# A fused transformer forward pass on one Trainium2 core: four transpositions of normalised rows, with the scale inside TensorE's product or in VectorE's copy

## The chip, the core and the metric

The kernel runs as one program on one core of one Trainium2 chip. The core has a matrix engine (TensorE, PE in the profile, with its weight loads listed apart as PEld), VectorE (DVE), ScalarE (ACT), GpSimd (POOL), and SyncE (SP), whose queue issues the transfers. Each engine runs its own list of instructions in order; semaphores tie the lists together. The metric is the device time of one execution in microseconds, lower is better. In this kernel about 0.2%, some 4 us, is what a measurement can tell from no change.

## The reference, cut to what matters

The program computes a first block (a mixer of convolutions and gates, cross attention, a mixture of 32 experts) and then a second block of two layers, for 256 tokens of width 1024, all in fp32. The four places that the change touches are the four RMS norms of the second block:

```python
def second_block(x, c, ada_w, ada_b, norm_gains, ...):
    for layer in range(2):
        shift_m, scale_m, gate_m, shift_f, scale_f, gate_f = ada_mod(c, ada_w[layer], ada_b[layer])
        h = modulate(rms_norm(x, norm_gains[layer, 0]), shift_m, scale_m)   # h0, h2
        y = attn_hybrid_mixer(h, ...) if layer % 2 == 0 else retention_mixer(h, ...)
        x = x + gate_m * y
        h = modulate(rms_norm(x, norm_gains[layer, 1]), shift_f, scale_f)   # h1, h3
        x = x + gate_f * swiglu(h, ffn_w_gate_up[layer], ffn_w_down[layer])
    return rms_norm(x, final_norm)
```

rms_norm divides every row (token) by the root of its mean square and multiplies by a gain per column; modulate multiplies by a factor and adds a shift per column.

## The kernel before, in words

The tokens lie in `x_tok`, 128 partitions by two row blocks i = 0, 1 by 1024 columns. The product after a norm needs the normalised tokens transposed: 8 chunks of 128 features on the partitions, 256 tokens along the free axis. This step is called a turn. There are seven: `t_mem`, `t_1`, `t_2` in the first block, and `t_h[0]` to `t_h[3]` (h0 to h3 here) at the part boundaries of the second block. Each turn is four groups, group 2i + h: row block i, half h of the columns, four 128x128 tiles in one PSUM bank.

`t_mem`, `t_1` and `t_2` turn rows that VectorE has normalised, by `pe.transpose` (L1089). h0 to h3 turn the rows of `x_tok` as they are and scale them in the same step: VectorE multiplies the identity by the column `inv[:, i]` of inverse roots (`scale_diag`, L2413, 128x128), and TensorE multiplies each tile by this diagonal matrix (L1087). The compiled fp32 product is two passes, 16 records in the trace for 8 tiles; a transposition has one.

Around it, at h1, h2 and h3, the list of each engine is this. VectorE, for the last block of tokens i: gate the product (L3037), add it to `x_tok` (L3042). ScalarE: the squares of the new half with their sum (L1751), the root (L1760). VectorE: the reciprocal (L2401), the diagonal (L2413). TensorE: the 8 tiles of block i. Then the turned tiles are read out of PSUM with the gain as factor and the shift added: ScalarE takes half h = 0 of block 0 (`turn_out`, L1772), VectorE half h = 1 (L2420). ScalarE makes the fp32r high part of h = 0 (L1713), VectorE the rest (L2319). Of block 1 ScalarE writes the high part of h = 0 straight from PSUM (`turn_out_last`, L1788), VectorE that of h = 1 (L2430). The first product of the next part (`first_units`, L978) takes ScalarE's chunks one by one as they land. L2312 and L1703 split weights into low and high parts and stand between these steps in both lists.

At h0 the rows come from the experts' sum: `finish_rows(i)` (L2867) writes `x_tok`, ScalarE takes the squares of whole rows (L1749) and the root, and in ScalarE's list a weight split (L1703) stands between the two row blocks. There ScalarE makes both high pieces of block 0 (L1713, twice), the second of which needs VectorE's L2420, before L1788.

TensorE waits for `tok_ready`, which VectorE raises by one for each row block. The turned tiles wait in banks `front`, freed by `evac`. Where `finish_rows` and `scale_diag` stand in VectorE's list is written out by hand at L2870 to L2877 for h0, and in `turn_scaled` (L3052) for the others.

Of the kernel before, what the change touches and what calls it, by code (L numbers as in the profile page):

```python
# [22 lines left out]
ALU = mybir.AluOpType  # L23
# [7 lines left out]
TT = T // P  # L31
# [162 lines left out]
def build_program(nc, a, consts1, consts2, decay, params, rows, gates_out, out):  # L194
    with ExitStack() as ctx:
# [5 lines left out]
        def sem(name):  # L201
            if name not in sems:
                sems[name] = ctx.enter_context(nc.semaphore(name))
            return sems[name]
# [45 lines left out]
        def big(i):  # L250
            return arena[:, i * DC * T:(i + 1) * DC * T].rearrange("p (c t) -> p c t", c=DC)
# [8 lines left out]
        def k1(name, n=P):  # L260
            return c1[:, C1[name]:C1[name] + n]

        ident = k1("ident")
        def tokens(i):
            return arena[:, i * DC * T:(i + 1) * DC * T].rearrange("p (i f) -> p i f", i=TT)

        x_tok, mem_tok = tokens(0), tokens(1)
# [107 lines left out]
        turn_h = [plan.turn()]  # L375
# [128 lines left out]
        def at(t):  # L504
            return ring[t.slot]
# [95 lines left out]
        inv, warm = small[:, 30:32], small[:, 63:64]  # L601
# [82 lines left out]
        def piece(x, k, pieces):  # L684

            if pieces == 1:
                return x
            if pieces == 2:
                n = x.shape[1] // 2
                return x[:, n * k:n * (k + 1), :]  # L690
            return x[:, 4 * (k % 2):4 * (k % 2) + 4, P * (k // 2):P * (k // 2 + 1)]
# [37 lines left out]
        def cols(name):  # L729
            return lambda c: pc(name, c)  # L730
# [3 lines left out]
        def mcol(layer, j):  # L734
            return lambda c: mod[:, 48 * layer + DC * j + c:48 * layer + DC * j + c + 1]

        def scol(k):
            return lambda c: gscale[:, DC * k + c:DC * k + c + 1]
# [1 line left out]
        t_mem = Turn(turn_mem, mem_tok, cols("mem_ln_g"), cols("mem_ln_b"), memT)  # L740
        t_1 = Turn(turn_1, tokens(8), cols("ln1_g"), cols("ln1_b"), x1T)
        t_2 = Turn(turn_2, tokens(8), cols("ln2_g"), cols("ln2_b"), x2T)
        inv_diag = [k1("before"), k1("slot")]
        t_h = [Turn(turn_h[k], x_tok, scol(k), mcol(k // 2, 3 * (k % 2)), big(6), inv_diag) for k in range(4)]

        def turned_part(t, i, h):

            g = t.block.groups[2 * i + h]
            return g, [(t.dst[:, 4 * h + k, P * i:P * (i + 1)], bank[g % BANKS][:, P * k:P * (k + 1)], 4 * h + k)
                       for k in range(4)]  # L750
# [203 lines left out]
        def _(pe):  # L954
            def open_group(g):
                if g >= BANKS:

                    pe.wait_ge(evac[g % BANKS], g // BANKS)
                return bank[g % BANKS]
# [115 lines left out]
            def turn(t, between=None):  # L1075

                for i in range(TT):
                    if i and between:
                        between()
                    pe.wait_ge(sem("tok_ready"), TT * t.n + i + 1)  # L1080
                    for h in range(2):
                        turned = open_group(t.block.groups[2 * i + h])
                        for k in range(4):
                            c = 4 * h + k
                            x, dst = t.src[:, i, c * P:(c + 1) * P], turned[:, k * P:(k + 1) * P]
                            if t.scale:
                                mm = pe.matmul(dst, x, t.scale[i], start=True, stop=True)  # L1087
                            else:
                                mm = pe.transpose(dst, x, ident)  # L1089
                        mm.then_inc(sem("mm_done"), 1)  # L1090

            def norm_mean(n):
# [70 lines left out]
            for k, g in enumerate(pool_groups):  # L1163
                dst = open_group(g)
                for i in range(TT):
                    for kc in range(2):
                        mm = pe.matmul(dst[:, i * T:(i + 1) * T], pool_in[:, 2 * k + kc, i * P:(i + 1) * P],
                                       at(pool_tile)[:, 2 * k + kc, 0:T], start=kc == 0, stop=kc == 1)
# [55 lines left out]
            for h in range(XHEADS):  # L1224
                wait_evac(pe, xq[h // 2].groups[h % 2])
                for i in range(TT):
                    for k in range(2):
                        mm = pe.matmul(bank[h][:, i * T:(i + 1) * T], qT[:, 2 * h + k, i * P:(i + 1) * P],
                                       kT[:, 2 * h + k, :], start=k == 0, stop=k == 1)
# [43 lines left out]
            def logits(i):  # L1273
# [3 lines left out]
                for k in range(DC):  # L1277
# [13 lines left out]
                      stop=True).then_inc(sem("r_pos"), 1)  # L1291
# [125 lines left out]
            for i in range(TT):  # L1417
                mm = pe.matmul(bank[5][0:NEXP, i * P:(i + 1) * P], gates[:, i, :], ident, start=True, stop=True)
# [875 lines left out]
        def _(dve):  # L2294
# [8 lines left out]
            V = nc.vector  # L2303
# [11 lines left out]
            def split_low(name, which=None):  # L2315
                first, pieces, src, high, low = splits[name]
                for k in which or range(pieces):
                    dve.wait_ge(sem("x_high"), first + k + 1)
                    V.tensor_tensor(piece(low, k, pieces), piece(src, k, pieces), piece(high, k, pieces).bitcast(F32),  # L2319
                                    ALU.subtract).then_inc(sem("x_split"), 1)  # L2320
# [76 lines left out]
            def invert(i):  # L2397

                inverses[0] += 1
                dve.wait_ge(sem("std"), inverses[0])  # L2400
                link(V.reciprocal(inv[:, i:i + 1], inv[:, i:i + 1]))  # L2401
# [5 lines left out]
                return V.tensor_scalar(dst[:, i, :], src[:, i, :], moments[:, i, 0:1], inv[:, i:i + 1],  # L2407
                                       ALU.subtract, ALU.mult)

            def scale_diag(t, i):  # L2410

                invert(i)
                V.tensor_scalar(t.scale[i], ident, inv[:, i:i + 1], None, ALU.mult).then_inc(sem("tok_ready"), 1)  # L2413

            def turn_out(t, i):

                g, parts = turned_part(t, i, 1)
                dve.wait_ge(sem("mm_done"), plan.done[g])
                for dst, ps, c in parts:
                    ins = V.tensor_scalar(dst, ps, t.g(c), t.b(c), ALU.mult, ALU.add)  # L2420
                ins.then_inc(evac[g % BANKS], 1)
# [293 lines left out]
            slot = k1("slot")  # L2715
# [71 lines left out]
            for q in range(4):  # L2787
                i, f = q // 2, slice((q % 2) * 512, (q % 2 + 1) * 512)
# [70 lines left out]
            def centre_late():  # L2859

                invert(1)
                link(V.scalar_tensor_tensor(out=acc[:, 1, :], in0=pair[1][:, :], scalar=late_neg, in1=g3,
                                            op0=ALU.add, op1=ALU.mult))

            def finish_rows(i):

                V.scalar_tensor_tensor(out=x_tok[:, i, :], in0=acc[:, i, :], scalar=inv[:, i:i + 1], in1=b3,  # L2867
                                       op0=ALU.mult, op1=ALU.add).then_inc(sem("resid"), 1)
# [2 lines left out]
            invert(0)  # L2871
            finish_rows(0)
            centre_late()
            scale_diag(t_h[0], 0)
            finish_rows(1)
            scale_diag(t_h[0], 1)
            turn_out(t_h[0], 0)  # L2877
            low_until(units_of(aq[0])[0])
            split_low("h0", (0,))
# [172 lines left out]
            def turn_scaled(t, name):  # L3052

                def then(i):
                    scale_diag(t, i)
                    if i:
                        turn_out(t, 0)
                        split_low(name, (0,))
                        turn_out_last(t, name)
                        split_low_last(t, name)  # L3060

                return then
# [245 lines left out]
```

## Time and profile before

| what | value |
|---|---|
| median of 3 runs | 2090.04 us |
| lowest and highest | 2089.27 and 2093.59 us |
| the profiled execution's own time | 2092.46 us |
| its span | 2090.7 us |
| PE busy in the span | 2022.1 us, 97% |
| DVE, ACT busy | 1126.7 us (54%), 708.4 us (34%) |
| mean granted clock of TensorE | 0.998 of full speed |

The span is the time between the first and the last instruction of the profiled execution; 1.8 us of its own time lie around it. The four boundaries lie at 1364 (h0), 1493 (h1), 1684 (h2) and 1892 us (h3). A granted clock (PEclk) of 1.00 is 2.4 GHz, 0.50 is 1.2 GHz. Ends of matmuls are modelled, and instructions of one engine overlap a little, so the start of the next may come before the end of the last.

### The profile page before, as it was taken

The numbers are of one execution on the slowest core, as the hardware profiler recorded it, in microseconds if no ns is written. First come the engines' busy times: TensorE is split into PE (matmuls) and PEld (weight loads), VectorE is DVE, ScalarE is ACT, GpSimd is POOL, SyncE is SP. The second block draws the span as 40 slices with busy tenths as digits, with TensorE's granted clock in tenths as the row PEclk, the third lists the DMA queues.
The fourth block names the chain that finished last, engine by engine and source line by source line (L and its number), as shares of the span: only waits on it lengthen the run. The fifth ranks groups of instructions, "written<-read, shape, count | busy, mean of one in ns | idle before, by whom it ended". The sixth has DMA issues, their size and how long they took to land.

```text
span 2090.7 us, 28509 instructions
## 1 busy us (share of the span) xinstructions
PE 2022.1 (97%) x11518; PEld 1339.9 (64%) x11518; DVE 1126.7 (54%) x1732; ACT 708.4 (34%) x937; POOL 3.1 (0%) x10
## 2 busy tenths in 40 slices
PE   8999999999999999999999999999999999999998
PEld 7999998853333333333333333388788898888887
DVE  6998898642222222221222222268798676657764
ACT  4334554521111111111111111175555443545543
POOL 0000000000000000000000000000000000000000
PEclk9999999999999999999999999999999999999999
DMA  9544759999999999999999999963488756646752
GB/s 340 190 170 174 282 200 368 364 392 396 429 428 427 428 428 429 429 428 429 427 429 428 428 429 427 419 234 111 150 289 283 262 189 215 211 161 202 249 173 81
DMA packets 188011, 654.91 MB, mean 313 GB/s; under 512 B 10992, under 2 KB 76528, under 8 KB 162704
## 3 DMA queue, kind: packets, MB, share of 16 engines
q1 hardware_dynamic: 187920, 653.59, 80.3%
q8 instruction: 71, 1.16, 0.2%
q14 instruction: 20, 0.16, 0.0%
HBM read 652.50 MB, written 1.06 MB: 313 GB/s over the span
## 4 chain that ended last, share of the span: by engine, by line
PE 74%; DMA 21%; DVE 3%; ACT 1%; issue 0%; SPq 0%; ACTq 0%; DVEq 0%
DMA ring<-w_down 21%; PE front L1020 19%; PE front L1071 15%; PE front L1322 10%; PE pair L1350 7%; PE front L1041 5%; PE pair L1041 2%; PE front L1043 2%; PE front L978 2%; PE pair L1390 1%; PE pair L1302 1%; PE pair L1043 1%; PE front L1332 1%; DMA ring<-w_in 1%; DVE ring_low L2312 1%; PE pair L1310 1%
## 5 line engine op out<-in xcount | busy, mean ns | idle before, releaser
L2312 DVE TENSOR_TENSOR ring_low<-ring,w_high 128x2048 fp32r<-128x2048 f32 (+1 forms) x179 | 404.6, 2266 | 133.0 <-ACT w_high L1703 132.5
L1322 PE MATMUL front<-ring,arena 128*64 128x512 f32 x1808 | 403.4, 595 | 9.9 <-DMA ring<-w_gu 9.7
L1703 ACT ACTIVATE w_high<-ring 128x2048 fp32r<-128x2048 f32 (+1 forms) x179 | 338.1, 1893 | 176.8 <-PE front L1071 77.9
L1020 PE MATMUL front<-x_parts,w_high 128*128 128x256 f32 x2048 | 373.5, 285 | 11.0 <-DVE ring_low L2512 9.1
L2808 DVE TENSOR_TENSOR arena<-front,par 128x512 f32<-128x512 f32 x64 | 44.0, 687 | 621.5 <-PE front L1332 621.5
L1020 PEld LDWEIGHTS front<-x_parts,w_high 128*128 128x128 f32 x2048 | 321.2, 193 | 14.7 <-issue 11.7
L1322 PEld LDWEIGHTS front<-ring,arena 128*64 128x64 f32 x1808 | 125.7, 137 | 278.3 <-issue 243.6
L1020 PE MATMUL front<-x_parts,ring_low 128*128 128x256 f32 x1024 | 290.6, 284 | 0.0
L1071 PE MATMUL front<-w_high,arena_r 128*128 128x512 f32 x736 | 229.2, 390 | 1.3 <-DVE ring_low L2312 0.7
L1350 PE MATMUL pair<-ring,arena 128*64 128x512 f32 x864 | 195.3, 597 | 27.5 <-DMA ring<-w_down 27.5
L1020 PEld LDWEIGHTS front<-x_parts,ring_low 128*128 128x128 f32 x1024 | 197.3, 193 | 0.0
L1071 PEld LDWEIGHTS front<-w_high,arena_r 128*128 128x128 f32 x736 | 138.2, 188 | 32.3 <-issue 3.1
L1350 PEld LDWEIGHTS pair<-ring,arena 128*64 128x64 f32 x864 | 59.3, 136 | 145.1 <-issue 145.1
L1041 PE MATMUL front<-x_parts,w_high 128*128 128x512 f32 x416 | 147.3, 398 | 0.0
L1071 PE MATMUL front<-ring_low,arena_r 128*128 128x512 f32 x368 | 143.3, 389 | 0.0
L1043 PE MATMUL front<-x_parts,ring_low 128*128 128x256 f32 x416 | 116.7, 280 | 0.0
L2017 ACT ACTIVATE arena<-front 128x512 f32<-128x512 f32 x64 | 34.7, 595 | 232.1 <-PE front L1322 232.1
L2362 DVE SCALAR_TENSOR_TENSOR arena<-a_pad,par,arena 128x256 f32<-128x256 f32 x240 | 98.5, 482 | 0.3
L2006 ACT ACTIVATE arena<-pair 128x512 f32<-128x512 f32 x32 | 19.1, 597 | 231.0 <-PE pair L1302 231.0
L1041 PEld LDWEIGHTS front<-x_parts,w_high 128*128 128x128 f32 x416 | 78.1, 188 | 20.4 <-issue 1.7
L2032 ACT ACTIVATE arena<-pair 128x512 f32<-128x512 f32 x30 | 17.9, 597 | 214.1 <-PE pair L1350 214.1
L1041 PE MATMUL pair<-x_parts,w_high 128*128 128x512 f32 x224 | 79.3, 397 | 0.0
(373 smaller groups left out, 2359.6 us busy)
## 6 DMA issues: line engine op xcount, KB each, us to landing
ring<-w_gu SPq DMA_DIRECT2D x113, 2048.0 KB, 23.6
ring<-w_down SPq DMA_DIRECT2D x57, 2048.0 KB, 25.4
ring<-ffn_w_gate_up SPq DMA_DIRECT2D x44, 1024.0 KB, 7.7
ring<-ada_w SPq DMA_DIRECT2D x20, 2048.0 KB, 8.7
ring<-ret_w_in SPq DMA_DIRECT2D x12, 2048.0 KB, 8.0
ring<-w_in SPq DMA_DIRECT2D x10, 2048.0 KB, 7.9
arena<-w_gu SPq DMA_DIRECT2D x10, 2048.0 KB, 15.4
ring<-ffn_w_down SPq DMA_DIRECT2D x8, 2048.0 KB, 8.3
```

The source lines that it names most:

```text
L978: mm = pe.matmul(acc_bank[:, ch * T:(ch + 1) * T], w[:, k, ch * P:(ch + 1) * P], xs[:, k, :], start=start and k + ch == 0, stop=stop and k ...
L1020: mm = pe.matmul(acc_bank[:, ch * T:(ch + 1) * T], w[:, k, ch * P:(ch + 1) * P], xs[:, kk, :], start=kk + ch + n == 0, stop=kk == b.kc - 1 ...
L1041: pe.matmul(both, high[:, k, cols], x_parts[:, :, k, :], start=k == 0, stop=False, skip_group_check=True)
L1043: mm = pe.matmul(sums[:, ch, :], low[:, k, cols], x[0][:, k, :], start=False, stop=k == b.kc - 1, skip_group_check=True)
L1071: mm = pe.matmul(acc_bank[:, :], xs[:, kk, i * P:(i + 1) * P], w[:, k, :], start=kk + n == 0, stop=kk == b.kc - 1 and n == 2)
L1322: mm = pe.matmul(bank[b][64 * o:64 * o + 64, :], xgT[:, k // 4, k % 4, :], gu_cols(b_in, j, D * o + 512 * b), start=k == 0, stop=k == DC - 1)
L1350: mm = pe.matmul(dst[64 * o:64 * o + 64, :], actT[:, k, :], down_cols(b_in, j, 512 * o), start=k == 0, stop=k == DC - 1)
L1703: nc.scalar.activation(high_part(u), raw_part(u), ACT.Copy).then_inc(sem("w_high"), 1)
L2017: nc.scalar.activation(gu_s[b], bank[b][:, :], ACT.Copy).then_inc(sem("m_gus"), 1)
L2312: V.tensor_tensor(low_part(u), raw_part(u), high_part(u).bitcast(F32), ALU.subtract).then_inc(sem("w_low"), 1)
L2362: V.scalar_tensor_tensor(out=conv[:, c, :], in0=a_pad[:, c, tap:tap + T], scalar=pc("conv_a_w", tap * DC + c), in1=conv[:, c, :], op0=ALU. ...
L2808: V.tensor_tensor(tv, bank[first + b][:, :].rearrange("p (c j) -> p c j", c=8), bias, ALU.add).then_inc(sem("m_vec"), 1)
```

## The change

The four boundaries turn scaled rows. `scale_rows` in place of `scale_diag` multiplies a row block of `x_tok` by `inv` into `tokens(2)`, in two halves of 512 columns, and raises `tok_ready` after each; `rows_ready` gives TensorE the count that it waits for before each group, and TensorE turns every tile by `pe.transpose`. At h0 `finish_rows(1)` moves ahead of both scalings. At h1, h2 and h3 VectorE's `turn_out(t, 0)` moves ahead of the scaling of block 1.

```diff
-        inv_diag = [k1("before"), k1("slot")]
-        t_h = [Turn(turn_h[k], x_tok, scol(k), mcol(k // 2, 3 * (k % 2)), big(6), inv_diag) for k in range(4)]
+        t_h = [Turn(turn_h[k], tokens(2), scol(k), mcol(k // 2, 3 * (k % 2)), big(6), x_tok) for k in range(4)]
+
+        def rows_ready(t, i, h):
+
+            if t.scale is None:
+                return TT * t.n + i + 1
+            return TT * t_h[0].n + 2 * TT * (t.n - t_h[0].n) + 2 * i + h + 1
...
-                    pe.wait_ge(sem("tok_ready"), TT * t.n + i + 1)
                     for h in range(2):
+                        pe.wait_ge(sem("tok_ready"), rows_ready(t, i, h))
                         turned = open_group(t.block.groups[2 * i + h])
...
-                            if t.scale:
-                                mm = pe.matmul(dst, x, t.scale[i], start=True, stop=True)
-                            else:
-                                mm = pe.transpose(dst, x, ident)
+                            mm = pe.transpose(dst, x, ident)
...
-            def scale_diag(t, i):
+            def scale_rows(t, i):
 
                 invert(i)
-                V.tensor_scalar(t.scale[i], ident, inv[:, i:i + 1], None, ALU.mult).then_inc(sem("tok_ready"), 1)
+                for h in range(2):
+                    cols = slice(512 * h, 512 * (h + 1))
+                    V.tensor_scalar(t.src[:, i, cols], t.scale[:, i, cols], inv[:, i:i + 1], None,
+                                    ALU.mult).then_inc(sem("tok_ready"), 1)
...
             centre_late()
-            scale_diag(t_h[0], 0)
             finish_rows(1)
-            scale_diag(t_h[0], 1)
+            scale_rows(t_h[0], 0)
+            scale_rows(t_h[0], 1)
             turn_out(t_h[0], 0)
...
                 def then(i):
-                    scale_diag(t, i)
                     if i:
                         turn_out(t, 0)
+                    scale_rows(t, i)
+                    if i:
                         split_low(name, (0,))
```

How this stands in VectorE's list at h0, from the row block 1 of the experts' rows to the weight split behind the turn. The names after the arrow are the tiles read; `c` holds the constants and the diagonals, `small` the inverse roots, `front` the turned tiles. Before:

```order
L2862 SCALAR_TENSOR_TENSOR arena<-pair,small,arena 128x1024 [waits dve_step]
L2401 RECIPROCAL small<-small 128x1 [waits std,dve_step]
L2413 TENSOR_SCALAR c<-c,small 128x128 [waits dve_step]
L2867 SCALAR_TENSOR_TENSOR arena<-arena,small 128x1024
L2401 RECIPROCAL small<-small 128x1 [waits std]
L2413 TENSOR_SCALAR c<-c,small 128x128 [waits dve_step]
L2420 TENSOR_SCALAR arena<-front,gscale,mod 128x128 [waits mm_done]
L2420 TENSOR_SCALAR arena<-front,gscale,mod 128x128 x3
L2312 TENSOR_TENSOR ring_low_52<-ring,w_high_53 128x8x256 [waits w_high]
```

and now (the lines of the changed kernel are three to six further down, L2418 is the scaling, L2873 `finish_rows`, L2426 `turn_out`, L2315 the weight split):

```order
L2868 SCALAR_TENSOR_TENSOR arena<-pair,small,arena 128x1024 [waits dve_step]
L2873 SCALAR_TENSOR_TENSOR arena<-arena,small 128x1024 [waits dve_step]
L2404 RECIPROCAL small<-small 128x1 [waits std]
L2418 TENSOR_SCALAR arena<-arena,small 128x512 [waits dve_step]
L2418 TENSOR_SCALAR arena<-arena,small 128x512
L2404 RECIPROCAL small<-small 128x1 [waits std]
L2418 TENSOR_SCALAR arena<-arena,small 128x512 [waits dve_step]
L2418 TENSOR_SCALAR arena<-arena,small 128x512
L2426 TENSOR_SCALAR arena<-front,gscale,mod 128x128 [waits mm_done]
L2426 TENSOR_SCALAR arena<-front,gscale,mod 128x128 x3
L2315 TENSOR_TENSOR ring_low_52<-ring,w_high_53 128x8x256 [waits w_high]
```

`finish_rows` stands ahead of the first reciprocal, and two copies of 128x512 for each row block stand where one of 128x128 did; ahead of `turn_out` there are now both copies of block 1.

VectorE's list at h1, from the addition of block 1 to the high part of its half. Before:

```order
L3042 TENSOR_TENSOR arena<-arena 128x512 [waits evacuated0]
L2401 RECIPROCAL small<-small 128x1 [waits std]
L2413 TENSOR_SCALAR c<-c,small 128x128 [waits dve_step]
L2420 TENSOR_SCALAR arena<-front,gscale,mod 128x128 [waits mm_done]
L2420 TENSOR_SCALAR arena<-front,gscale,mod 128x128 x3
L2319 TENSOR_TENSOR x_parts<-arena,x_parts 128x4x128 [waits x_high]
L2430 TENSOR_SCALAR x_parts<-front,gscale,mod 128x128 [waits x_split,mm_done]
```

and now (L3048 is the addition, L2322 the low part, L2436 the high part):

```order
L3048 TENSOR_TENSOR arena<-arena 128x512 [waits evacuated0]
L2426 TENSOR_SCALAR arena<-front,gscale,mod 128x128 [waits mm_done]
L2426 TENSOR_SCALAR arena<-front,gscale,mod 128x128 x3
L2404 RECIPROCAL small<-small 128x1 [waits std]
L2418 TENSOR_SCALAR arena<-arena,small 128x512 [waits dve_step]
L2418 TENSOR_SCALAR arena<-arena,small 128x512
L2322 TENSOR_TENSOR x_parts<-arena,x_parts 128x4x128 [waits x_high]
L2436 TENSOR_SCALAR x_parts<-front,gscale,mod 128x128 [waits x_split,mm_done]
```

The four reads out of PSUM stand ahead of the reciprocal and the scalings. h2 and h3 have the same rows with other bank numbers. TensorE's list has the same 16 tiles in the same order at each boundary, with a wait for `tok_ready` before each group of four in place of one before each eight.

## Rows read from the trace of the kernel before

**Rows 1.** The page, busy time (share of the span) of each engine, TensorE and VectorE
```profile
PE 2022.1 (97%) x11518; PEld 1339.9 (64%) x11518; DVE 1126.7 (54%) x1732; ACT 708.4 (34%) x937; POOL 3.1 (0%) x10
```

**Rows 2.** Chain of waits, 1492 to 1500: start us, us, what
```profile
1496.10 2.05 PE front L1087 x16
1498.15 1.91 PE front L978 x12
```

**Rows 3.** Timeline, boundary h1: start us, us, engine, line, operation [idle before <-releaser]
```profile
1492.83 1.95 PE L1087 MATMUL front<-c,arena 128*128 128x128 f32 x16
...
1493.75 0.69 DVE L3042 TENSOR_TENSOR arena<-arena 128x512 f32<-128x512 f32 x1
...
1495.43 1.49 ACT L1772 ACTIVATE arena<-front,mod,gscale 128x128 f32<-128x128 f32 x4
1495.56 0.16 DVE L2401 RECIPROCAL small<-small 128x1 f32<-128x1 f32 x1 [1.11 <-ACT small L1760]
...
1496.10 2.05 PE L1087 MATMUL front<-c,arena 128*128 128x128 f32 x16 [1.33 <-DVE c L2413]
1497.01 0.63 ACT L1713 ACTIVATE x_parts<-arena 128x512 fp32r<-128x512 f32 x1
1497.55 1.49 ACT L1788 ACTIVATE x_parts<-front,mod,gscale 128x128 fp32r<-128x128 f32 x4
...
1498.13 1.46 PE L978 MATMUL front<-x_parts,w_high 128*128 128x256 f32 x8
1498.28 1.36 DVE L2430 TENSOR_SCALAR x_parts<-front,gscale,mod 128x128 fp32r<-128x128 f32 x4
```

**Rows 4.** Timeline, boundary h2
```profile
1689.11 1.50 ACT L1788 ACTIVATE x_parts<-front,mod,gscale 128x128 fp32r<-128x128 f32 x4
...
1689.69 1.47 PE L978 MATMUL front<-x_parts,w_high 128*128 128x256 f32 x8
```

**Rows 5.** Timeline, the turn t_1 and the products before it
```profile
347.93 1.92 PE L1119 MATMUL pair<-ring,silu_c 128*32 128x512 f32 x16
...
351.80 1.09 PE L1089 MATMUL front<-c,arena 128*128 128x128 f32 x8
```

**Rows 6.** Line L3129: duration ns min/median/max, first and last start, form
```profile
L3129 DVE TENSOR_SCALAR arena<-arena,small x2: 485/487/489, 2083.0 to 2087.0; 128x512 f32<-128x512 f32 x2
```

**Rows 7.** Timeline, boundary h0
```profile
1367.19 0.29 DVE L2413 TENSOR_SCALAR c<-c,small 128x128 f32<-128x128 f32 x1
1367.39 1.36 DVE L2420 TENSOR_SCALAR arena<-front,gscale,mod 128x128 f32<-128x128 f32 x4
...
1368.44 1.15 ACT L1713 ACTIVATE x_parts<-arena 128x512 fp32r<-128x512 f32 x2
1368.67 2.29 DVE L2312 TENSOR_TENSOR ring_low<-ring,w_high 128x2048 fp32r<-128x2048 f32 x1
1369.50 1.49 ACT L1788 ACTIVATE x_parts<-front,mod,gscale 128x128 fp32r<-128x128 f32 x4
...
1370.08 1.46 PE L978 MATMUL front<-x_parts,w_high 128*128 128x256 f32 x8 [0.50 <-ACT x_parts L1788]
```

**Rows 8.** Chain of waits, boundary h0
```profile
1368.98 0.61 ACT x_parts L1713
```

**Rows 9.** Stretches around turn t_2: busy of each engine, PEclk, DMA share, GB/s
```profile
436.00:440.00 4.00, 4.00 (x25) 4.00 (x24) 2.81 (x4) 1.44 (x2) 0.00 (x0) 0.60 1.00 426
440.00:443.00 3.00, 3.00 (x17) 1.45 (x21) 1.80 (x13) 0.00 (x0) 0.00 (x0) 0.50 1.01 426
443.00:446.00 3.00, 3.00 (x21) 1.79 (x14) 2.72 (x10) 1.02 (x3) 0.00 (x0) 0.90 0.95 322
```

**Rows 10.** Timeline of PE, turn t_2 and the router's products
```profile
433.95 1.09 PE L1089 MATMUL front<-c,arena 128*128 128x128 f32 x8 [0.42 <-DVE arena L2407]
435.32 5.67 PE L1278 MATMUL pair<-par,arena 128*128 128x32 f32 x32 [0.28 <-DVE arena L2420]
440.92 3.24 PE L1119 MATMUL pair<-ring,silu_c 128*32 128x512 f32 x16
```

## Prediction

> **What bounds the kernel now.** I began with the busy shares on the page: TensorE is busy for 97% of the span [rows 1]. So a change pays only where it makes TensorE start earlier or work less, and at the four boundaries the question is who lets it start again. The chain of waits at h1 runs through the add of block 1, its squares and root, the reciprocal and the diagonal into TensorE's 16 passes, 2.05 us, and from these straight into the first product L978 [rows 2]. By the chain alone, those passes are on the path.
>
> The timeline beside it says otherwise. ScalarE's row of the same moments is closed: the four reads of block 0 start at 1495.43, the high part at 1497.01, the four high chunks of block 1 at 1497.55, and L978 at 1498.13 [rows 3]. L978 starts 0.58 us after ScalarE's L1788. At h2 it is 1689.69 - 1689.11 = 0.58 [rows 4], and at h0, where TensorE does stand idle for ScalarE and is therefore surely not the last, 1370.08 - 1369.50 = 0.58 [rows 7]. The same distance where TensorE is free and where the chain blames it means that ScalarE is the last link at h1 and h2 too, and TensorE's passes end level with it by chance. I read h3 as h2. So at each boundary the path is: add, squares, root, then 2.7 us of ScalarE reads (1495.43 to 1498.13 at h1). Nothing in the change shortens these.
>
> **The change part by part.**
>
> *TensorE's tiles.* A group of 8 tiles takes 1.95 to 2.05 us as products of two passes [rows 3]; 8 transpositions take 1.09 us [rows 5]. Removed work: 8 groups x 0.9 to 0.96, about 7.5 us of busy time. What of it is on the path? The first group of each boundary ends at 1494.78 before and TensorE then waits 1.33 us for block 1 [rows 3]; it will only wait longer. The second group starts when block 1 is scaled and must be half done when ScalarE comes to it at 1497.55, and wholly done at 1498.13. Both hold now. Worth: 0, and between 0 and 0.96 us at each of h1 to h3 if my reading of ScalarE is wrong.
>
> *VectorE's copies at h1 to h3.* The diagonal of 128x128 goes, two copies of 128x512 come. The same form is in L3129, 0.49 us [rows 6]. For block 0: reciprocal, two copies, done about 0.7 us later than the diagonal was, still before TensorE finishes the last product of the part at 1492.8. Hidden. For block 1: VectorE's add ends at 1493.75 + 0.69 = 1494.44 [rows 3]. Now its four reads (1.36 us, the form at 1367.39 [rows 7]) come first and end about 1495.75, where it would else have idled 1.11 us [rows 3]. The reciprocal, before at 1495.56, moves to about 1495.65. First copy done at 1496.35, second at 1496.85. Half a group of transpositions is 0.6 us: the first four tiles are ready at 1497.0, the others at 1497.4. ScalarE wants the first at 1497.55, VectorE the others at 1498.28, TensorE wants to be free at 1498.13. Spare: 0.5, 0.8 and 0.7 us. Worth: 0; the cover is gone when a copy takes over 0.49 + 0.25 us.
>
> *VectorE at h0.* Here the reads stand behind the copies. `finish_rows(1)` moves 0.6 us forward, but the squares of block 1 stand behind a weight split in ScalarE's list, so the second reciprocal stays at 1367.0. Before, the diagonal starts at 1367.19 and the reads at 1367.39, a step of 0.20 [rows 7]. Two copies step 0.40 to 0.49 each, so the reads start 0.6 to 0.8 us later, at 1368.0 to 1368.2, and end 1369.35 to 1369.55. ScalarE's second high piece, 1368.98 before [rows 8], needs them: it slips by 0.4 to 0.6 us, and with it L1788 and L978. The weight split L2312 slips by the same 0.6 to 0.8 from its 1368.67, ends near 1371.6, and the products that need it start near 1371.85. Cost: +0.4 to +0.6, taken +0.5. If ScalarE is then still later than I think it is 0; if VectorE's high chunks (4 x 0.34) come late as well, +0.8.
>
> *Waits.* Each group of four tiles has its own wait, 14 more in seven turns, all on a count that in `t_mem`, `t_1` and `t_2` has already been reached. Behind them stand only TensorE's own tiles. A step over a semaphore takes up to 0.09 us (L1772 ends at 1496.92, L1713 starts at 1497.01 [rows 3]), so between 0 and 14 x 0.09 = 1.3 us; the count being reached already, taken 0. SP's and the other queues wait for the same `mm_done` counts and lose nothing.
>
> *TensorE's clock.* The removed passes were work that TensorE did in the gap. After the change it does, between the last product at 1492.83 and L978 at 1498.13, two groups of 1.09 us in 5.3 us, where it did 4.0 us; at h0 about 2.2 in 6.5. One place of the trace before resembles this: the turn `t_2`. TensorE turns 8 tiles at 433.95, waits 0.28 us, then does narrow products (32 columns) from 435.32 [rows 10], and the granted clock falls in 436 to 440 (mean 0.60), is 0.50 in 440 to 443 and 0.90 in 443 to 446 [rows 9]. That is 3.2 + 3.0 + 0.6 = 6.8 us at 1.2 GHz. It came back 2.7 us after wide products had begun again at 440.92 [rows 10]. Turn `t_1`, with products of 512 columns around its transpositions, kept 2.4 GHz. The price of the low level: the 16 products of L1119 take 3.24 us at 440.92 and 1.92 us at 347.93 [rows 5, 10], 1.32 lost in some 2.7 low, 0.49 us per us. After a boundary the products are wide at once, so what matters is the low time behind L978: from 0 to those 6.8 us, 0 to 3.3 us per fall. I take 1.5 us low, under the 2.7 of the row since part of it lies before L978: 0.7 us. And I take it at three of four boundaries, +2.1.
>
> On this the Trainium skill has a sentence (TensorE: Matmul & The Clock Gate, Part 4: PE-mode transpose): a transposition does not count as PE-busy the way a product does. It speaks against this change, and `t_2` agrees with it [rows 9, 10], though the narrow products stand there as well. By the page all four boundaries would look idle to the gate: four falls, +2.8 in place of +2.1.
>
> **The sum.** h1 to h3 0; h0 +0.5; waits 0; clock +2.1; together +2.6 us. The profiled execution took 2092.46 us, 1.8 over its span of 2090.7, so a like one gives 2095.1. It stands 2.4 above the median of 2090.04; on that median the forecast is 2092.6.
>
> **The rivals.**
>
> 1. *The clock stays up.* For it: no gap of TensorE at a boundary is as empty as the router's stretch is long, and in the trace before the clock holds at all four. Against: the removed passes are what held it. Then only h0's +0.5 remains, 2090.5.
>
> 2. *Slower: the clock falls at all four and stays low as long as in rows 9.* Place: the products behind L978. Price 6.8 x 0.49 = 3.3 us each, 13.3 + 0.5, 2103.9. It decides, that is passes 4 us in all, from 1.8 us low behind L978 at each boundary. For it: that length is the only one that the trace shows within the program. Against: there TensorE stayed on narrow products for 5.67 of the 6.8 us.
>
> 3. *Faster: the chain is right.* The passes of block 1 are the last link at h1, h2 and h3, and L978 starts as much earlier as they shrink, 3 x 0.96 = 2.9 us less, h0's +0.5 kept: 2087.6. For it: the chain of waits, which shows no idle time before L978. Against: 0.58 us three times. A further gain cannot come, since the root of block 1 does not move.
>
> 4. *The copies don't hold their place.* A 128x512 copy that took 0.8 us instead of 0.49 would bring the first tiles of block 1 at 1497.3 and the others at 1498.0: still just hidden at h1 to h3, but +1.2 at h0: 2091.2.
>
> **How the numbers follow.** The forecast with falls at some boundaries 0.50; rival 1 0.27; rival 2 0.11, most of it well under its full price; rival 3 0.07; rival 4 0.05. A difference under 0.2%, 4.2 us, can't be told from none here. Rival 3 reaches faster only with the spread of the runs (2089.27 to 2093.59), so faster gets 0.06. Rival 2 is slower, and the forecast with long falls gives a little: slower 0.15. Same 0.79. The range must hold that spread of 4.3 us around terms of -2.4 to +6: 2088.0 to 2096.8; rival 2 at its full price is left out.
>
> **What would show it.** Right: L978 starts 0.58 us after L1788 at all four boundaries, and in h1 to h3 L1788 starts as long after the add as before (3.8 us); TensorE shows two idle gaps per boundary, the longer about 2.5 us; at h0 ScalarE's second high piece waits for VectorE's reads and L978 comes 0.5 us later after the weight split; PEclk is below 1.00 in some of the stretches behind a boundary. Wrong: L1788 or L978 nearer to the add by half a microsecond (rival 3), PEclk 1.00 throughout (rival 1), or ScalarE or VectorE waiting for a group of block 1 at h1 to h3 (copies slower than taken). The forecast as a whole is wrong if the median moves by over 4 us in either direction.

## The result, and the profile after

| kernel | runs | median us | ratio to before, 95% interval |
|---|---|---|---|
| before | 17 | 2090.04 (2088.67 to 2093.59) | |
| changed | 17 | 2094.65 (2090.70 to 2096.42) | 1.0020 (1.0013 to 1.0026) |

The change made the kernel 4.6 us, 0.22%, slower. That is just above the 0.2% that I set as the bound of "same", over the 4 us at which I had called the forecast as a whole wrong, and inside the range. The profiled execution took 2092.84 us (span 2091.0, mean granted clock 0.995; before 2092.46, 2090.7 and 0.998).

TensorE has fewer passes, as intended. The page of the changed kernel, against [rows 1]:

```profile
PE 2017.0 (96%) x11454; PEld 1334.1 (64%) x11454; DVE 1131.1 (54%) x1740; ACT 709.0 (34%) x937; POOL 3.1 (0%) x10
```

5.1 us less busy time, and a longer run. The timeline at h1, which answers to [rows 3] (the lines are three to six further down; the columns are the same):

```profile
1491.09 1.03 PE L1092 MATMUL front<-c,arena 128*128 128x128 f32 x8
...
1492.02 0.69 DVE L3048 TENSOR_TENSOR arena<-arena 128x512 f32<-128x512 f32 x1
...
1494.09 0.88 DVE L2418 TENSOR_SCALAR arena<-arena,small 128x512 f32<-128x512 f32 x2
...
1494.63 1.09 PE L1092 MATMUL front<-c,arena 128*128 128x128 f32 x8 [2.51 <-DVE arena L2418]
...
1495.82 1.49 ACT L1791 ACTIVATE x_parts<-front,mod,gscale 128x128 fp32r<-128x128 f32 x4
...
1496.40 1.46 PE L984 MATMUL front<-x_parts,w_high 128*128 128x256 f32 x8 [0.67 <-ACT x_parts L1791]
```

From the add (L3048) to the first product (L984) it is 1496.40 - 1492.02 = 4.38 us. Before it was 1498.13 - 1493.75 = 4.38. TensorE now stands idle for 2.51 us where it did for 1.33. The chain of waits over the same stretch no longer names TensorE's tiles (start, us, what), against [rows 2]:

```profile
1493.79 1.41 ACT arena L1775 x4
...
1495.82 0.45 ACT x_parts L1791
...
1496.40 1.70 PE front L984 x10
```

With the passes gone the chain goes through ScalarE's reads, and the end of it has not moved. At h1 to h3 the difference is behind the first product. The granted clock is the number ahead of the last two (DMA share and GB/s); stretches of h0 (two), h1, h2 and h3:

```profile
1364.00:1370.00 6.00, 5.03 (x22) 4.66 (x23) 6.00 (x13) 5.60 (x14) 0.00 (x0) 0.51 1.05 389
1370.00:1376.00 6.00, 6.00 (x49) 6.00 (x48) 6.00 (x9) 2.85 (x2) 0.00 (x0) 0.92 0.55 220
1498.00:1504.00 6.00, 6.00 (x52) 6.00 (x52) 6.00 (x9) 4.31 (x6) 0.00 (x0) 1.00 0.13 39
1690.00:1696.00 6.00, 6.00 (x46) 6.00 (x45) 6.00 (x8) 2.61 (x4) 0.00 (x0) 0.85 0.01 4
1898.00:1904.00 6.00, 6.00 (x45) 6.00 (x44) 6.00 (x12) 5.44 (x9) 0.00 (x0) 0.83 0.33 106
```

Before, all five read 1.00. Now the clock is at 1.2 GHz for (1 - 0.51) x 2 x 6 = 5.9 us and 1.0 us more at h0, 6.8 in all, for none at h1, and for 3.4 us each at h2 and h3 (from stretches of 1 us). What it costs shows in how far the block of 48 products lies behind the first product: the distance at full clock is 4.17 to 4.18 us before. At h2 after:

```profile
1687.39 1.49 ACT L1791 ACTIVATE x_parts<-front,mod,gscale 128x128 fp32r<-128x128 f32 x4
...
1687.97 1.83 PE L984 MATMUL front<-x_parts,w_high 128*128 128x256 f32 x8 [0.67 <-ACT x_parts L1791]
...
1693.43 5.92 PE L984 MATMUL front<-x_parts,w_high 128*128 128x256 f32 x48
```

and before, whose first product is in [rows 4]:

```profile
1693.87 5.92 PE L978 MATMUL front<-x_parts,w_high 128*128 128x256 f32 x48
```

5.46 us against 4.18: 1.28 lost, and the first product still 0.58 us behind ScalarE's L1791. At h0, against [rows 7]:

```profile
1364.16 1.97 PE L1092 MATMUL front<-c,arena 128*128 128x128 f32 x8 [1.00 <-DVE arena L2418]
...
1365.82 0.63 ACT L1716 ACTIVATE x_parts<-arena 128x512 fp32r<-128x512 f32 x1 [0.31 <-DVE arena L2426]
1366.36 1.49 ACT L1791 ACTIVATE x_parts<-front,mod,gscale 128x128 fp32r<-128x128 f32 x4
...
1366.94 2.05 PE L984 MATMUL front<-x_parts,w_high 128*128 128x256 f32 x8 [0.81 <-ACT x_parts L1791]
...
1372.59 5.92 PE L984 MATMUL front<-x_parts,w_high 128*128 128x256 f32 x48
```

and before:

```profile
1374.25 5.99 PE L978 MATMUL front<-x_parts,w_high 128*128 128x256 f32 x48
```

ScalarE's second high piece waited 0.31 us for VectorE's reads. From the start of `finish_rows(0)` (1357.43 now, 1360.87 before) to the first product it is 9.51 us where it was 9.21, so 0.30 lost; from there to the 48 products 5.65 where it was 4.17, 1.48 lost. About 0.1 of the 1.48 is not the clock's: in e5 and e8 below, whose clock stays up at h0, that distance is 4.26 and 4.28. The clock fell at 1364.1, ahead of the second group, which took 1.97 us where the first took 1.09. Of this one profile:

| | h0 | h1 | h2 | h3 | sum |
|---|---|---|---|---|---|
| first product later | 0.30 | 0 | 0 | 0 | 0.30 |
| products behind it slower | 1.48 | 0 | 1.28 | 0.83 | 3.59 |

3.9 us. The span grew by only 0.3 mostly because the experts' stage ended 3.4 us earlier in this execution (L1368's last products at 1352.5, L1365's before at 1355.9), 1.9 of it already at its start: the clock, low for 6.8 us at `t_2` in [rows 9], was low for half of that here (PEclk 0.88 in 436 to 440, 0.58 in 440 to 443). That stage varies from run to run by itself.

### The profile page after: what moved, and what is told of

Same layout as the page of the kernel before. It is cut to its first block, busy times and chain, and to the rows that moved or that the text cites. A ratio compares the mean times of both kernels' runs of the same rounds, so it can differ in the third digit from the quotient of the medians.

```text
span 2091.0 us, 28402 instructions
## 1 busy us (share of the span) xinstructions
PE 2017.0 (96%) x11454; PEld 1334.1 (64%) x11454; DVE 1131.1 (54%) x1740; ACT 709.0 (34%) x937; POOL 3.1 (0%) x10
## 4 chain that ended last, share of the span: by engine, by line
PE 74%; DMA 21%; DVE 2%; ACT 1%; issue 0%; SPq 0%; ACTq 0%; DVEq 0%
DMA ring<-w_down 21%; PE front L1026 19%; PE front L1077 15%; PE front L1325 10%; PE pair L1353 7%; PE front L1047 5%; PE pair L1047 2%; PE front L984 2%; PE front L1049 2%; PE pair L1393 1%; PE pair L1305 1%; PE pair L1049 1%; PE front L1335 1%; DMA ring<-w_in 1%; DVE ring_low L2315 1%; PE pair L1122 1%
## 5 line engine op out<-in xcount | busy, mean ns | idle before, releaser
L2315 DVE TENSOR_TENSOR ring_low<-ring,w_high 128x2048 fp32r<-128x2048 f32 (+1 forms) x179 | 404.7, 2267 | 137.3 <-ACT w_high L1706 136.8
```

What stands on the lines that cost most here:

```text
L2315: V.tensor_tensor(low_part(u), raw_part(u), high_part(u).bitcast(F32), ALU.subtract).then_inc(sem("w_low"), 1)
```

## The experiments

Theory 1: TensorE's clock falls, since the removed passes leave it too little to do between the two parts. Theory 2: VectorE's copies and their new place cost the time. All times are medians; each ratio is to runs of the kernel before on the same chip, whose medians were 2090.23 (beside e1 to e8), 2089.90 (e9 to e11) and 2089.64 us (e12). The low times are those of the one profiled execution.

| kernel | median | ratio (95%) | clock low at h0, h1, h2, h3, us |
|---|---|---|---|
| e1_products | 2094.28 | 1.0020 (1.0011 to 1.0029) | 0, 3.4, 0, 3.4 |
| e2_raw_turn | 2095.45 | 1.0020 (1.0011 to 1.0030) | 6.8, 3.4, 3.4, 6.8 |
| e3_fill | 2094.07 | 1.0016 (1.0007 to 1.0025) | none |
| e4_fill_h0 | 2093.68 | 1.0016 (1.0007 to 1.0025) | none |
| e5_fill_fit | 2090.27 | 1.0001 (0.9992 to 1.0010) | none |
| e6_fill_fit_h0 | 2089.84 | 1.0001 (0.9992 to 1.0010) | none |
| e7_early_reads | 2088.77 | 0.9993 (0.9984 to 1.0002) | none |
| e8_products_order | 2091.83 | 1.0009 (1.0000 to 1.0018) | none |
| e9_early_one_fill | 2088.29 | 0.9991 (0.9982 to 1.0000) | none |
| e10_turn_fill | 2092.14 | 1.0014 (1.0003 to 1.0026) | none |
| e11_changed_again | 2094.98 | 1.0020 (1.0011 to 1.0029) | 6.8, 0, 3.4, 6.8 |
| e12_turn_fill_again | 2092.92 | 1.0018 (1.0006 to 1.0031) | none |

**e2: the transpositions alone.** The kernel before with one line changed; the norm's scale is left out of the result.

```diff
-                                mm = pe.matmul(dst, x, t.scale[i], start=True, stop=True)
+                                mm = pe.transpose(dst, x, ident)
```

> The kernel before with VectorE's list untouched (the diagonal is still made and waited for), but TensorE turns the unscaled rows by transposition at the four boundaries; the norm's scale is left out of what is computed. Theory 1: the clock falls at two to four boundaries, +2.5 to +4.5 us over before, 2092.5 to 2094.5, though nothing was added to VectorE. Theory 2: TensorE's shorter tiles cost nothing, 2090.0; by the chain of waits (TensorE's passes last at h1 to h3) it would be 2.9 us less, 2087.1.

Measured 2095.45, 5.2 us over before and above the range that I gave theory 1, with VectorE's list untouched. TensorE stood idle for 2.24 us between the groups at h1 to h3, where the kernel before has 1.33. The first product stands 4.38 us behind the add at h1, h2 and h3 (4.39), as before; the clock falls at all four boundaries. The stretches behind h2 and at h3:

```profile
1690.00:1696.00 6.00, 6.00 (x39) 5.95 (x39) 6.00 (x12) 4.38 (x8) 0.00 (x0) 0.72 0.30 111
1898.00:1904.00 6.00, 5.06 (x26) 4.85 (x24) 5.65 (x15) 5.89 (x13) 0.00 (x0) 0.54 0.64 209
```

From first product to the 48 it is 6.04, 4.48, 5.51 and 6.56 us against 4.17 to 4.18: 5.9 us lost in the profile. At h1 only 0.31 was lost, since 2.2 of the 3.4 us at the low clock lay before the first product. Theory 2 gave 2090.0 and is out as the main cause, and the chain's promise of 2087.1 too.

The clock was lower in the other executions too, not only in the profiled ones: its mean over an execution was 0.993 to 0.997 (median 0.994) in the 17 of the changed kernel and in the 10 of e2, and 0.996 to 0.999 (median 0.998) in those of the kernel before beside the experiments. The shortest of each, 2090.70 and 2090.09 us, are the ones with 0.997.

**e1: the copies, with products.** The tiles of h0 to h3 as two-pass products with the identity, the rest as changed.

```diff
-                            mm = pe.transpose(dst, x, ident)
+                            if t.scale is None:
+                                mm = pe.transpose(dst, x, ident)
+                            else:
+                                mm = pe.matmul(dst, x, ident, start=True, stop=True)
```

> The changed kernel with its scaled copies and its order in VectorE's list, but at the four boundaries TensorE turns the tiles by a two-pass product with the identity in place of a transposition. Theory 1 (the time was lost because TensorE's clock falls when its tiles in the gap are transpositions): no fall at any boundary, each L978-like first product 0.57 to 0.58 us behind ScalarE's first high chunk; only the later start at h0, 0.3 us, stays: 2090.0 to 2091.0 us where before is 2090.0. Theory 2 (the copies and their order cost the time): unchanged against the changed kernel, about 2094.6.

A miss: 2094.28, which by itself is what theory 2 forecast. But the experiment had a fault of its own, which its timeline at h1 shows:

```profile
1489.15 1.95 PE L1095 MATMUL front<-c,arena 128*128 128x128 f32 x16
...
1491.14 1.37 DVE L2429 TENSOR_SCALAR arena<-front,gscale,mod 128x128 f32<-128x128 f32 x4 [0.37 <-PE front L1095]
...
1493.15 3.28 PE L1095 MATMUL front<-c,arena 128*128 128x128 f32 x16 [2.05 <-DVE arena L2421]
...
1494.76 1.50 ACT L1794 ACTIVATE x_parts<-front,mod,gscale 128x128 fp32r<-128x128 f32 x4 [0.79 <-PE front L1095]
...
1496.08 1.67 PE L984 MATMUL front<-x_parts,w_high 128*128 128x256 f32 x8
```

VectorE's reads, now ahead of the scaling, wait 0.37 us for the longer group of block 0 and make the scaling late; TensorE idles 2.05 us, the clock falls although its tiles are products, and the second group takes 3.28 us where it took 2.05. The first product is 6.00 us behind the add (4.88 at h2, which did not fall, and 5.35 at h3). So products in the group are not enough; the empty time between the groups matters as well.

**e8: the same with the old order.** As e1, and `scale_rows` ahead of `turn_out` at h1 to h3.

```diff
                 def then(i):
+                    scale_rows(t, i)
                     if i:
                         turn_out(t, 0)
-                    scale_rows(t, i)
-                    if i:
                         split_low(name, (0,))
```

> The scaled copies of the changed kernel with two-pass products with the identity in place of the transpositions, and at h1 to h3 the order of the kernel before (the scaling ahead of turn_out). In the run with products and the new order TensorE waited 2.05 us for block 1 and the clock fell at h1 and h3; with the old order it waits about 1.5 us. Theory 1: no fall, the copies alone cost 0.2 to 0.3 us at each boundary since TensorE's two-pass group becomes the last link: 2090.8 to 2091.6. Theory 2: 2094.

```profile
1493.06 2.05 PE L1095 MATMUL front<-c,arena 128*128 128x128 f32 x16 [1.53 <-DVE arena L2421]
...
1494.31 1.49 ACT L1794 ACTIVATE x_parts<-front,mod,gscale 128x128 fp32r<-128x128 f32 x4
...
1494.89 1.46 PE L984 MATMUL front<-x_parts,w_high 128*128 128x256 f32 x8
```

No fall, idle time 1.53 us, the first product 4.38 us behind the add: the copies cost nothing at h1 to h3, even ahead of the reads. The profile accounts for 0.4 us at h0 (0.30 to the first product, 0.11 behind it); the median is 1.6 up with an interval that begins at 1.0000, so the rest isn't settled.

**e3, e4: the gaps filled, too long.** Unread products behind each row block's tiles.

```diff
                         mm.then_inc(sem("mm_done"), 1)
+                    if t.scale is not None:
+                        for _ in range(1 if i else 2 if t is t_h[0] else 5):
+                            pe.matmul(bank[4], ident, c1[:, 0:COLS], start=True, stop=True)
```

> The changed kernel, and behind each row block's transpositions at h0 to h3 TensorE does products of 128x512 that nobody reads, into a bank that is free: 5 behind block 0 (2 at h0), 1 behind block 1, 2.15 us and 0.43 us in gaps of 2.5 and 0.67 us. Theory 1: the clock stays at 2.4 GHz at h1 to h3, and perhaps at h0, where less fits: 2090.3 if at all four, 2091.7 if h0 still falls. Theory 2: no less than the changed kernel, 2094.6, and more where a product overlaps the start of the next part.

> As the filled kernel, and at h0 VectorE's reads out of PSUM (turn_out) stand ahead of the scaling of block 1, as at the other boundaries. Both theories: ScalarE's second high piece no longer waits for VectorE, so the first product at h0 starts 0.4 us earlier, slightly ahead of the kernel before (0.1 us). Theory 1: 2089.9 us together. Theory 2: 2094.2.

Both miss, 2094.07 and 2093.68, and both keep the clock at all four boundaries:

```profile
1493.69 4.46 PE L1096 MATMUL pair<-c 128*128 128x512 f32 x10
...
1497.98 1.04 PE L1092 MATMUL front<-c,arena 128*128 128x128 f32 x8
...
1498.62 1.50 ACT L1794 ACTIVATE x_parts<-front,mod,gscale 128x128 fp32r<-128x128 f32 x4 [0.99 <-PE front L1092]
...
1499.32 1.52 PE L984 MATMUL front<-x_parts,w_high 128*128 128x256 f32 x8
```

A 512-column product takes 0.89 us, twice what I had reckoned (I counted one of its two passes), and five of them hold TensorE to 1498.15. The first product is 5.57 to 5.58 us behind the add, 1.2 later at each of three boundaries, 3.6 us: what the clock gave back went there. In e4, which also has the change at h0 that e6 has, the first product there comes 0.32 us earlier than in the changed kernel.

**e5, e6: the gaps filled to measure.** 256 columns in place of 512; e6 also moves `turn_out` ahead of `scale_rows(t_h[0], 1)` at h0.

```diff
-                            pe.matmul(bank[4], ident, c1[:, 0:COLS], start=True, stop=True)
+                            pe.matmul(bank[4][:, 0:T], ident, c1[:, 0:T], start=True, stop=True)
```

> The changed kernel with shorter unread products behind the transpositions: 256 columns each, two passes of 0.22 us, 5 behind block 0 (2 at h0) and 1 behind block 1. The 512-column ones of the first try took 0.89 us each, 4.46 us for five, and held TensorE past its second group. Theory 1 (the clock): these end within the gaps of 2.51 and 0.67 us, the clock stays at 2.4 GHz at all four, L984 stands 4.38 us behind the add at h1 to h3 as before, and only h0's later start stays: 2090.0 to 2091.2. Theory 2 (copies and order, not the clock): 2094 as before.

```profile
1492.24 2.32 PE L1096 MATMUL pair<-c 128*128 128x256 f32 x10
...
1494.91 1.09 PE L1092 MATMUL front<-c,arena 128*128 128x128 f32 x8 [0.35 <-DVE arena L2421]
...
1496.09 1.49 ACT L1794 ACTIVATE x_parts<-front,mod,gscale 128x128 fp32r<-128x128 f32 x4
...
1496.67 1.46 PE L984 MATMUL front<-x_parts,w_high 128*128 128x256 f32 x8 [0.23 <-ACT x_parts L1794]
```

```profile
1364.00:1370.00 6.00, 4.63 (x31) 3.70 (x30) 4.96 (x10) 5.57 (x15) 0.00 (x0) 1.00 1.05 386
1690.00:1696.00 6.00, 6.00 (x52) 6.00 (x51) 6.00 (x9) 2.88 (x5) 0.00 (x0) 1.00 0.03 11
1898.00:1904.00 6.00, 6.00 (x52) 6.00 (x52) 6.00 (x9) 4.33 (x6) 0.00 (x0) 1.00 0.14 44
```

2090.27, against 2090.23 of the kernel before on its chip: of the changed kernel's 4.6 us nothing is left that can be told from chance (the interval allows 2 us either way). TensorE idles 0.35 us before its second group, the clock reads 1.00, and every copy, wait and reordering of the change is still in. This is the run that shows the cause, with e2 as its mirror. Its mean clock is 0.997 to 0.999 (median 0.998) in its 11 runs, as before.

> As the kernel with fitted products, and at h0 VectorE's reads stand ahead of the scaling of block 1. Theory 1: 0.3 us less, level with the kernel before, 2089.7 to 2090.7. Theory 2: 2094.

2089.84. At h0 the first product stands 9.09 us behind `finish_rows(0)`, 0.42 less than in the changed kernel and 0.12 less than before; the 48 products behind it stand 13.57 us from there, where it was 13.38, since VectorE's later steps now come late. The medians differ by 0.4, which they can't tell from chance; the profile can.

**e7, e9: a version that uses the shorter tiles.** e7 is e6, and ScalarE does three reads of block 0 ahead of the squares of block 1; e9 is e7 without the unread product behind block 1 at h1 to h3.

```diff
             def turn_rms(t, name):
 
+                turn_out(t, 0, range(3))
                 sum_squares(1, 1)
                 rms_root(1)
-                turn_out(t, 0)
+                turn_out(t, 0, (3,))
```

> As that one, and ScalarE does three of its four reads of block 0 (turn_out) at h1 to h3 ahead of the squares of block 1, in the 1.2 us in which it waits for VectorE's add. My reading that ScalarE is the last link: its list after the root shrinks by 3 x 0.37 us, then the second group's transpositions bound it, so the first product starts 0.5 us earlier at h1, h2 and h3, 1.5 us in all: about 2088.6. If VectorE and TensorE are the last link: no gain, 2090.2.

```profile
1493.11 1.16 ACT L1778 ACTIVATE arena<-front,mod,gscale 128x128 f32<-128x128 f32 x3 [0.21 <-PE front L1092]
...
1493.39 0.69 DVE L3053 TENSOR_TENSOR arena<-arena 128x512 f32<-128x512 f32 x1
...
1495.10 0.44 ACT L1778 ACTIVATE arena<-front,mod,gscale 128x128 f32<-128x128 f32 x1
...
1496.01 1.09 PE L1092 MATMUL front<-c,arena 128*128 128x128 f32 x8 [0.35 <-DVE arena L2423]
...
1496.70 1.51 ACT L1796 ACTIVATE x_parts<-front,mod,gscale 128x128 fp32r<-128x128 f32 x4 [0.44 <-PE front L1092]
...
1497.31 1.46 PE L984 MATMUL front<-x_parts,w_high 128*128 128x256 f32 x8
```

ScalarE now waits 0.44 us for TensorE's second group (the bracket of L1796), and the first product is 3.92 us behind the add in place of 4.38, at h2 and h3 too (3.91, 3.92). So ScalarE had been the last link. The early reads need block 0 turned early, which transpositions do 0.9 us sooner than products; what early reads would give with the products of the kernel before was not run.

2088.77, near the forecast, with an interval of 0.9984 to 1.0002.

> The version with early reads, without the unread product behind block 1 at h1 to h3: there it ended at 1497.54 and the first product started at 1497.31, 0.61 us behind ScalarE's first high chunk where 0.57 to 0.58 is usual. First product 3.9 us behind the add as there, or 0.03 less. Theory 1: clock up at all four (the products behind block 0 stand), 2088.0 to 2089.0, level with the version with early reads. Theory 2 has no view of it.

2088.29 (2086.59 to 2090.93) against 2089.90: 1.6 us faster than before and 6.7 us faster than the changed kernel on the same chip (e11, 2094.98). The interval ends at 1.0000, so against before it is likely and no more.

**e10, e12: filled with transpositions.** 18 of them behind block 0 and 3 behind block 1 (7 and 3 at h0), about as long as the products of e5 (2.13 us for 2.32 behind block 0).

```diff
-                            pe.matmul(bank[4][:, 0:T], ident, c1[:, 0:T], start=True, stop=True)
+                            pe.transpose(bank[4][:, 0:P], c1[:, 0:P], ident)
```

> The changed kernel, its gaps filled as in the fitted version, but with unread transpositions (0.12 us each; 18 behind block 0 and 3 behind block 1, 7 and 3 at h0) in place of products. It tells apart two forms of theory 1. If transpositions do not count as activity, the clock falls as in the changed kernel though TensorE has no gap: two to four boundaries in the profile, 2093.5 to 2095. If only idle time counts, no fall, 2090.0 to 2091.0.

```profile
1492.25 2.13 PE L1096 MATMUL pair<-c 128*128 128x128 f32 x18
...
1494.91 1.09 PE L1092 MATMUL front<-c,arena 128*128 128x128 f32 x8 [0.54 <-DVE arena L2421]
...
1496.68 1.46 PE L984 MATMUL front<-x_parts,w_high 128*128 128x256 f32 x8 [0.35 <-ACT x_parts L1794]
```

```profile
1364.00:1370.00 6.00, 4.42 (x35) 3.87 (x34) 4.96 (x10) 5.57 (x15) 0.00 (x0) 1.00 1.05 387
1690.00:1696.00 6.00, 6.00 (x52) 6.00 (x51) 6.00 (x9) 2.89 (x5) 0.00 (x0) 1.00 0.04 11
1898.00:1904.00 6.00, 6.00 (x52) 6.00 (x52) 6.00 (x9) 4.33 (x6) 0.00 (x0) 1.00 0.15 46
```

The clock stays at 1.00 at all four boundaries with nothing but transpositions in the gap. The median of 2092.14 lies between the two ranges that I had given, and 4 of 11 times lay above 2095. The same kernel a second time:

> The gaps filled with unread transpositions once more, since its first profile had no fall at any of four boundaries but 4 of its 11 times lay above 2095, where the version filled with products had none above 2093.8. If transpositions hold the clock: no fall in this profile, median 2090 to 2091.5. If they hold it only at some positions in time: falls at one or two boundaries, median 2092 to 2093.

No fall at a boundary in this profile either, eight of eight in all. Its time was 2095.62, and the trace says where: between h2 and h3 the 48 products and the add lie 206.3 us apart, in e10 199.6.

```profile
1777.45 0.49 DVE L2919 TENSOR_SCALAR spare<-ring,silu_c 128x512 f32<-128x512 f32 x1 [12.91 <-DMA ring<-ada_w]
```

```profile
1793.37 1.71 PE L1647 MATMUL pair<-arena,cv_pad 128*128 128x512 f32 x2 [4.71 <-ACT arena L2242]
```

VectorE waited 12.91 us for a tile of `ada_w` (5.3 to 9.4 in the other profiles), which made the group norm late, and TensorE stood for 4.71 us; behind that its clock was low for 3.4 us. That is a late transfer and not a turn. Six of the 12 times lie at 2090.1 to 2091.3, six at 2094.5 and above; the median of 2092.92 misses the range that I gave for no fall, and why the late ones are so many in e10 and e12 stays open.

**e11: the changed kernel again.**

> The changed kernel itself once more, for a second profile and more runs beside the others. Theory 1: falls at two to four boundaries, which need not be the same ones (the first profile had them at h0, h2 and h3, the one of raw transposed rows at all four), and a median of 2093.5 to 2095. Theory 2: the same time without a tie to the clock.

2094.98, with 6.8, 0, 3.4 and 6.8 us of low clock and 0.30 + 1.57 + 0 + 1.33 + 2.38 = 5.6 us lost. With the first profile's 3.9 the mean is 4.7, and the medians are 4.6 and 5.1 above before. The clock term and h0's 0.4 account for all of it.

## Why the prediction was right, and what it mis-sized

- *TensorE's tiles, ScalarE the last link at h1 to h3: right.* 4.38 us from add to first product before and after, L984 0.58 to 0.59 us behind L1791, the idle gap at h1 to h3 2.51 us as forecast. e7 shows it from the other side. The chain of waits had named an engine that ended level by chance.
- *VectorE's copies: right.* A copy steps 0.40 us, the reads at h0 came late and held ScalarE for 0.31 us. I took +0.5, it was +0.30 to the first product and +0.4 to the 48 (13.77 us from `finish_rows(0)` in e5, 13.38 before); hidden at h1 to h3 (e8). What I had not seen is that `finish_rows(1)`, moved ahead, makes the first group at h0 wait 1.54 us where it waited 0.33.
- *Waits: right at 0 as far as e5 can tell*, which has them all and is level with before within 2 us.
- *Clock: the mechanism right, its size wrong.* I took 0.7 us per fall with 1.5 us at the low level behind the first product, three falls, +2.1. The falls measured 0.83, 1.28 and 1.33 us where the clock was low for 3.4 us, and 1.48, 1.57 and 2.38 where it was low for 6.8; summed 3.6 and 5.3 in two profiles. The mis-sized term is "I take 1.5 us low". Behind the first product the clock was low for 4.0, 3.4 and 2.5 us (h0, h2, h3) in one profile and for 4.2, 3.4 and 6.0 in the other (from stretches of 0.2 us). I had taken the 2.7 us of the row as the most and cut it, because a part lies before L978; but at h2 the fall began 0.4 us behind the first product, so that no part lay before it, and at h3 6.0 us passed under wide products before the clock came back. The price per us was too high instead: 0.34 to 0.40 us lost per us low where I had 0.49. Three falls of four, which I had taken without a row that says three, came so in both profiles; that is luck, e2 has four.
- *The sum.* +0.3 and some +4.4 in place of +0.5 and +2.1, 2094.65 in place of 2092.6. I gave 0.79 to a difference under 0.2% and 0.15 to slower; it came out at the edge of the two, and by my own sign (over 4 us) the forecast as a whole failed by 0.6 us. What came lies between the forecast and rival 2, whose long fall was there at one boundary of four in one profile and at two in the other. The range held because it was made for the spread of the runs and for longer falls.
- *The page.* The Trainium skill (TensorE: Matmul & The Clock Gate, Part 4: PE-mode transpose) says that a transposition doesn't count as PE-busy the way a product does. I drew on it, and for the fall it sided with what came. e10 and e12 do not agree with the rule as put: a gap filled with transpositions alone kept 2.4 GHz at eight boundaries of eight. And e1 fell with products. What goes with the falls is empty time around short groups, but no length of a gap divides the rows. At h1 to h3 the clock fell behind a gap of 2.05 us at two boundaries of three (e1), of 2.24 at three of three (e2) and of 2.51 at four of six (the changed kernel twice, never at h1), and never with 1.33 (before), 1.53 (e8), 0.35 (e5) and 0.54 us (e10). At h0 it fell in both profiles of the changed kernel with gaps of only some 1.54, 1.00 and 0.81 us around its two groups, and did not in e8 with products and gaps of 1.54 and 0.73, nor in e10 with 1.54, 0.23 and 1.35. In e2 the transpositions did not only count less, if they do, they ended 0.9 us sooner and left the gap of 2.24 us. Whether a transposition counts for somewhat less than a product these runs don't settle.

## What to carry to other kernels

An engine's time saved inside a gap is not saved: ask first who ends the gap, and read that from a place where the suspected engine is free (here 0.58 us behind ScalarE at h0 as at h1). When TensorE's work between two dense stretches is cut, look at the granted clock behind the gap; a fall cost 0.8 to 2.4 us in the changed kernel where the cut could bring 0.96 at most, and cheap products that nobody reads held the clock here (e5), provided that they end before the next wait does (e3 and e4 show the other case). A shortened step pays when its reader is moved to meet it, as ScalarE's reads in e7 and e9.

## What the runs showed of the hardware that I had not expected

- TensorE's clock fell to 1.2 GHz at boundaries with gaps of 2.05 to 2.51 us beside short groups of tiles, and at h0 with gaps of 1.54, 1.00 and 0.81 us, and stayed there for 3.4 or 6.8 us while dense products ran; the same kernel fell at other boundaries, or for longer, in another execution (h3: 3.4 us in one profile, 6.8 in the next; h1 in neither).
- An fp32 product of 128x128 by 128x512 is two records of 0.45 us each; a transposition of 128x128 is one of 0.12 us.
- A 2 MB transfer of `ada_w`, usually 5.3 to 9.4 us late for VectorE without harm, was 12.9 us late in one execution (e12), in which that stretch was 6.7 us longer than in e10; how much of the spread of these runs comes from it was not measured.
